# Choosing the experts token tile by token tile, in front of the first tile's last split steps

## The reference, cut to what matters

```python
hf = rmsnorm(x, norm_ffn_g[layer])
logits = (xt @ w_router + b_router).astype(jnp.float32)
top_vals, top_idx = lax.top_k(logits, TOP_K)
gates = jax.nn.softmax(top_vals, axis=-1)
...
gu = xb @ w1[e] + b1[e]
gate = jnp.minimum(gu[:, :F], SWIGLU_LIMIT)
up = jnp.clip(gu[:, F:], -SWIGLU_LIMIT, SWIGLU_LIMIT)
act = (up + 1.0) * gate * jax.nn.sigmoid(SWIGLU_ALPHA * gate)
return act @ w2[e] + b2[e]
```

## Time and profile before

| what | us |
|---|---|
| median of 3 runs | 1243.93 |
| the 3 runs, lowest and highest | 1243.72 and 1245.78 |
| the profiled execution | 1244.29 |
| its span, first to last instruction | 1242.5 |
| PE busy in the span | 1172.0 |
| DVE busy in the span | 373.4 |

### The profile page before, as it was taken

The page is one execution under the profiler, slowest core; times in us unless marked ns, Lnnn a source line. Parts: engine busy times, 40 slices in busy tenths (PEclk is TensorE's granted clock), DMA queues, the critical chain, the costliest instruction groups (busy, mean ns, idle before and its releaser), DMA issues.

```text
span 1242.5 us, 17266 instructions
## 1 busy us (share of the span) xinstructions
PE 1172.0 (94%) x7208; PEld 591.8 (48%) x7208; DVE 373.4 (30%) x677; ACT 228.8 (18%) x342; POOL 58.5 (5%) x39
## 2 busy tenths in 40 slices
PE   9999999999999999999988999999999999989997
PEld 8998888888633333333333333333333333333332
DVE  5655755656522112121111112211112111111112
ACT  5444543544510001000000001000000000000001
POOL 0950000000300000000000000000000000000000
PEclk9999999999999999999999999999999999999999
DMA  9755435947999999999999999999999999999996
GB/s 311 265 203 183 156 136 207 353 152 282 370 422 429 426 429 427 428 428 430 427 428 429 429 428 427 429 430 428 426 430 429 428 428 428 429 430 428 427 426 268
DMA packets 56644, 461.88 MB, mean 372 GB/s; under 512 B 5665, under 2 KB 7394, under 8 KB 31682
## 3 DMA queue, kind: packets, MB, share of 16 engines
q1 hardware_dynamic: 53096, 457.99, 88.8%
q10 hardware_dynamic: 3514, 3.40, 0.9%
HBM read 460.30 MB, written 1.07 MB: 371 GB/s over the span
## 4 chain that ended last, share of the span: by engine, by line
PE 58%; DMA 37%; DVE 1%; SPq 1%; ACT 1%; issue 0%; POOL 0%; DVEq 0%; ACTq 0%
DMA w_ring<-in_w 23%; PE ps L1211 15%; PE ps L1261 11%; DMA behind_xb<-in_w 7%; DMA behind_watt<-in_w 7%; PE ps L1347 3%; PE ps L948 3%; PE ps L946 3%; PE ps L947 3%; PE ps L1189 2%; PE ps L939 2%; PE ps L942 2%; PE ps L941 2%; SPq L553 1%; PE ps L958 1%; PE ps L1084 1%
## 5 line engine op out<-in xcount | busy, mean ns | idle before, releaser
L1211 PE MATMUL ps<-w_ring,A_W 128*64 128x512 f32 x1232 | 278.7, 597 | 32.8 <-DMA w_ring<-in_w 32.5
L1211 PEld LDWEIGHTS ps<-w_ring,A_W 128*64 128x64 f32 x1232 | 84.3, 136 | 204.1 <-issue 141.9
L1757 DVE TENSOR_SCALAR A_W<-ps 128x512 f32<-128x512 f32 x32 | 22.1, 692 | 499.1 <-PE ps L1211 499.1
L1261 PE MATMUL ps<-w_ring,A_W 128*64 128x512 f32 x592 | 134.2, 595 | 0.0
L1424 DVE TENSOR_TENSOR w_parts<-w_ring,w_parts 128x1024 fp32r<-128x1024 f32 x76 | 101.8, 1349 | 86.3 <-ACT w_parts L657 86.0
L853 ACT ACTIVATE A_W<-A_W 128x512 f32<-128x512 f32 x32 | 20.2, 630 | 526.9 <-DVE A_W L1757 526.9
L1211 PE MATMUL ps<-A_QK,A_W 128*64 128x512 f32 x416 | 94.8, 597 | 9.9 <-DMA A_QK<-in_w 9.9
L657 ACT ACTIVATE w_parts<-w_ring 128x1024 fp32r<-128x1024 f32 x76 | 80.1, 1059 | 73.3 <-PE ps L948 37.8
L1261 PEld LDWEIGHTS ps<-w_ring,A_W 128*64 128x64 f32 x592 | 40.3, 136 | 68.6 <-issue 66.9
L857 ACT ACTIVATE A_W<-ps 128x512 f32<-128x512 f32 x31 | 18.5, 597 | 290.8 <-PE ps L1242 290.8
L946 PE MATMUL ps<-w_parts,hT_hi 128*128 128x512 f32 x176 | 69.4, 394 | 0.0
(11 more groups left out here) (255 smaller groups left out, 1263.8 us busy)
## 6 DMA issues: line engine op xcount, KB each, us to landing
w_ring<-in_w SPq DMA_DIRECT2D x113, 2048.0 KB, 43.7
A_QK<-in_w SPq DMA_DIRECT2D x38, 2048.0 KB, 42.8
behind_watt<-in_w SPq DMA_DIRECT2D x19, 2048.0 KB, 43.7
w_ring<-in_w_in SPq DMA_DIRECT2D x36, 1024.0 KB, 7.1
behind_xb<-in_w SPq DMA_DIRECT2D x18, 2048.0 KB, 43.7
w_ring<-in_w_ret_branch SPq DMA_DIRECT2D x2, 2048.0 KB, 12.3
w_ring<-in_w SPq DMA_DIRECT2D x4, 1024.0 KB, 40.1
A_W<-in_w_out SPq DMA_DIRECT2D x1, 2560.0 KB, 14.3
```

What stands on the lines that cost most here:

```text
L1211: mm = pe.matmul(o, XT[:, k, :], tile[:, j, c * HALF:(c + 1) * HALF], start=(k == 0), stop=(k == KC - 1))
L1261: mm = pe.matmul(ps[CAP * c:CAP * c + CAP, 3, :], lhs, w2_tile(flat)[:, q % W2_ROWS, c * HALF:(c + 1) * HALF], start=False, stop=(q == FQ ...
```

## The change

On DVE the choice of experts is made for one tile at a time, and tile 0's choice is put in front of `first_rest(2)` and `first_rest(3)`, which stay in front of tile 1's. The two masks are signalled one by one, and PE's position counts wait for both. The reduction to `mask_f` and the steps behind it stay joint for both tiles. On PE tile 1's logits begin as soon as the first four column blocks are copied, and eight fill matmuls in front of them go. The tile `chosen` moves to words 5888 to 6143 of A_W, away from words 4096 to 4351, which tile 1's transposed columns (xT[1]) still hold at that time.

```diff
-        chosen = A_W[:, 4096:4096 + TT * TOP_K * N_EXP].rearrange("p (t j e) -> p t j e", t=TT, j=TOP_K)
+        chosen = A_W[:, 5888:5888 + TT * TOP_K * N_EXP].rearrange("p (t j e) -> p t j e", t=TT, j=TOP_K)
...
             logits(0, range(4, KC)).then_inc(s_lg, 1)
-            fill(1, 8)
+            pe.wait_ge(s_xte, 3)
+            logits(1, range(4))
             pe.wait_ge(s_xte, 4)
-            logits(1, range(KC)).then_inc(s_lg, 1)
+            logits(1, range(4, KC)).then_inc(s_lg, 1)
             fill(2, 30)
 
-            pe.wait_ge(s_mask, 1)
+            pe.wait_ge(s_mask, TT)
...
             residual_scale(1)
+
+            lg = [top[:, 32 + t * 32:64 + t * 32] for t in range(TT)]
+            best = top[:, 0:16].rearrange("p (t j) -> p t j", t=TT)
+
+            def choose_experts(t):
+                dve.wait_ge(s_lg, t + 1)
+                link(dve.scalar_tensor_tensor(lg[t], ps[:, t, 0:N_EXP], rstd[:, t:t + 1], br_sb[:, :], ALU.mult, ALU.add))
+                link(dve.max(best[:, t, :], lg[t]))
+                link(dve.max_index(ids[:, t, :].bitcast(U32), best[:, t, :], lg[t]))
+                experts = expert_sb[:, :].rearrange("p (a e) -> p a e", a=1).broadcast_to([P, TOP_K, N_EXP])
+                owners = ids[:, t, 0:TOP_K].bitcast(U32).rearrange("p (j a) -> p j a", a=1).broadcast_to([P, TOP_K, N_EXP])
+                link(dve.tensor_tensor(chosen[:, t], experts, owners, ALU.is_equal))
+                dve.tensor_reduce(mask_bf[:, t, :], chosen[:, t].rearrange("p j e -> p e j"), AX.X, ALU.max).then_inc(s_mask, 1)
+
+            choose_experts(0)
             first_rest(2)
             first_rest(3)
-
-            lg = [top[:, 32 + t * 32:64 + t * 32] for t in range(TT)]
-            best = top[:, 0:16].rearrange("p (t j) -> p t j", t=TT)
-            for t in range(TT):
-                dve.wait_ge(s_lg, t + 1)
-                last = dve.scalar_tensor_tensor(lg[t], ps[:, t, 0:N_EXP], rstd[:, t:t + 1],
-                                                br_sb[:, :], ALU.mult, ALU.add)
-            link(last)
-            for t in range(TT):
-                last = dve.max(best[:, t, :], lg[t])
-            link(last)
-            for t in range(TT):
-                last = dve.max_index(ids[:, t, :].bitcast(U32), best[:, t, :], lg[t])
-            link(last)
-            experts = expert_sb[:, :].rearrange("p (a b e) -> p a b e", a=1, b=1).broadcast_to([P, TT, TOP_K, N_EXP])
-            owners = ids[:, :, 0:TOP_K].bitcast(U32).rearrange("p t (j a) -> p t j a", a=1).broadcast_to([P, TT, TOP_K, N_EXP])
-            link(dve.tensor_tensor(chosen, experts, owners, ALU.is_equal))
-            dve.tensor_reduce(mask_bf[:, :, :], chosen.rearrange("p t j e -> p t e j"), AX.X, ALU.max).then_inc(s_mask, 1)
+            choose_experts(1)
             dve.tensor_reduce(mask_f, chosen.rearrange("p t j e -> p t e j"), AX.X, ALU.max).then_inc(s_maskf, 1)
```

## The result

The changed kernel takes 1252.78 us, median of 4 runs (1252.33 to 1252.90), against 1244.14 for the kernel before, median of 4. The medians lie 8.6 us apart, and the measured ratio is 1.0064 with a 95% interval of 1.0052 to 1.0077. The forecast was no change, at 1244.7.

The account below looks back on a forecast made before the run. The full DMA weight stream from unit 10 on was taken as the bound. A store 0.94 us later, less 0.14 filled by the gain's transfer, gave +0.8 us on 1243.93, so 1244.7 us, range 1243.4 to 1245.6.

Parts of the forecast that it names:

- The bound: Weight stream: from unit 10 on only DMA fixes the end; 381.7 MB at 429 GB/s need 889.7 us.
- Nothing else moves.: Outside the routing stage: new place of `chosen` costs no time, SP's queue and the loop stay the same.
- The collisions: Routing stage: DVE's two-input instructions and POOL's exclude each other, store 0.94 us later, 1244.7 us in all; chance 0.50.
- my estimate of 0.28: DVE, routing stage: one tile's comparison over 128 columns takes 0.28 us, upper bound 0.64.
- my 1.54: DVE, routing stage: one tile's choice of experts takes 1.54 us undisturbed, 321.29 to 322.83 for tile 0.
- The clock rival: PE idle 3.3 us before the counts: clock falls, expert 0's first unit takes twice 3.65 us, 1248.4 us; chance 0.04.
- My condition: PE before the counts: clock can fall only after a wait longer than 2.06 us, mask later than 326.2.
- The asymmetry: PE's start of expert 0: earlier gains at most 0.3 us, later costs nearly the full slip.
- The hole: DMA stream before unit 10: gap of some 0.3 us grows by 0.94, less 0.14 filled by the gain's transfer.
- My signs: Profile after: right if the later rate is 427 to 430 GB/s; wrong if granted clock under 1.00 between 327 and 340.
- "Within 0.2%": Whole kernel: time stays within 0.2%, or 2.5 us, of before; chance 0.95, slower 0.04, faster 0.01.
- All rivals: Routing stage: undisturbed 1243.8 us (0.40), fallen PE clock 1248.4 (0.04), whole 0.84 us gained 1243.1 (0.04).

Follow-up runs that it names:

- e5: Kernel before with 24 extra matmuls of 512 columns on ones in each round of PE's expert loop; 1244.29 us, ratio 1.0004.
- e1: Changed kernel with eight more matmuls on ones at the start of PE's program, restoring the loop's old place; 1243.76 us, ratio 1.0001.
- e2: Kernel before with eight fewer matmuls on ones at the start of PE's program, loop at its new place; 1252.55 us, ratio 1.0067.
- e10: Kernel before with 60 memory-to-memory copies of 16 KB, spread over all DMA engines, in ACT's expert loop; 1246.35 us, ratio 1.0019.
- e11: Kernel before with 30 undivided copies of one row of 4099 words in ACT's expert loop; 1259.76 us, ratio 1.0125.
- e4: Changed kernel with the eight fills put back behind tile 1's logits, in PE's idle time; 1243.98 us, ratio 1.0003.
- e3: Changed kernel with only DVE's part kept: PE has its eight fills and tile 1's logits in one piece again; 1244.14 us, ratio 1.0001.
- e6: Kernel before with 48 more matmuls on ones at the start of PE's program; 1244.33 us, ratio 1.0004.
- e8: Kernel before with one matmul on ones fewer at the start of PE's program; 1252.80 us, ratio 1.0071.
- e9: Kernel before with 80 more matmuls on ones at the start of PE's program; 1253.93 us, ratio 1.0074.
- e7: Kernel before with 64 more matmuls on ones at the start of PE's program; 1248.92 us, four runs from 1244.78 to 1251.59.

## Why the prediction was wrong, point by point

**The bound was right.** The DMA stream fixes the end from unit 10 on. e5 confirms it: 15 us more work of PE in 450 us, and no change.

**The step that failed** is the sentence "Nothing else moves. [...] SP's queue and the loop are the same." The loop's code is the same, but its place in PE's program is not. The term was left out altogether: 45 more loads of PE instructions in a stream with no room. e1 and e2 show it from both sides, the loss gone with the place restored, and 8.5 us there with nothing but the place changed. The row on queue 8 stood in the page of before: 26 packets, 0.43 MB, which is PE's built program loaded once although its loop runs six times. I did not ask what keeps a loop of 1670 instructions loaded, nor what would end it.

**The size, worked out.** In the loop the weights fall behind. From 350 to 1200 us the weights' queue and queue 8 moved, in the kernel before and in the changed one:

```profile
q1 hardware_dynamic: 24992, 363.90, 100.6%
q8 instruction: 7, 0.11, 0.1%
```

```profile
q1 hardware_dynamic: 24869, 362.11, 100.2%
q8 instruction: 52, 0.85, 0.4%
```

That is 1.79 MB less of weights for 0.74 MB more of instructions. Over sixteen engines at 429 GB/s 1.79 MB are 4.2 us, which is also what 427 in place of 429 GB/s makes of 381.7 MB (893.9 us against 889.7, both rates rounded). But the end of the stream shows eight engines late and eight in time. Eight engines bring half of 429 GB/s, and at that rate 1.79 MB are 8.3 us, close to the 8.6 measured. That the 45 loads lie on those eight is an inference from the shares of the last windows, since the profile gives a packet no engine. What stays open is why a load displaces 2.4 times its own bytes. In the time of an engine a load costs 8.6 x 8 / 45 = 1.5 us, an undivided copy of the same size 0.52 (15.6 / 30). So its size alone does not explain its price, and e10 and e11 show only that the spread over engines matters (0.04 us a copy, 2.2 / 60, when spread).

**The collisions** were right in kind and three times too large. Timeline of DVE and of POOL in the changed kernel:

```profile
322.53 2.31 DVE L1650 SCALAR_TENSOR_TENSOR A_W<-A_W,small,xs 128x512 f32<-128x512 f32 x2
...
325.56 0.44 DVE L1673 TENSOR_TENSOR A_W<-expert_sb,A_W 128x128 f32<-128x128 f32 x1
```

```profile
322.93 4.09 POOL L614 TENSOR_TENSOR A_W<-A_W,xs 128x512 f32<-128x512 f32 x3 [0.87 <-ACT xs L804]
```

The two first rests took 2.31 us in place of 1.45, 0.86 more, which I read as a wait of one of them for POOL. POOL's three rests took 4.09 in place of 3.77, 0.32 more and not 0.94. I had laid `first_rest(3)` and the comparison end to end with POOL's jobs in full; POOL gave up only 0.32 for both. Tile 1's comparison took 0.44 us beside these rests, over my estimate of 0.28, but far from a wait for a whole job of POOL. Tile 0's choice took 1.69 us (320.93 to 322.62) against my 1.54.

**The clock rival**, at 4 in 100, came true as a mechanism: the mask came after 2.58 us of idle PE and the clock was at its lower level through the gather, 2.74 us in place of 1.57. Its price was wrong. The clock was back when expert 0 began, whose first unit took 3.65 us as before; what it cost was the gather's 1.17 us. Between e1 and e4, where the clock held, no loss can be measured: 1243.76 and 1243.98. My condition, a wait longer than 2.06 us, did not decide either: the clock held after 2.13 (e4) and fell after 2.15 (e3).

**The asymmetry** of the store, hidden if earlier, paid if later, could not be tested finely. The hole that I forecast as 0.8 us is there: from 333 to 338 the changed routing stage brings 300 GB/s (e1) and the old one 372 (e2), a difference of 5 x 72 / 429 = 0.8 us.

```profile
333.00:338.00 5.00, 5.00 (x28) 1.77 (x26) 2.24 (x14) 1.04 (x2) 0.00 (x0) 1.00 0.90 300
```

```profile
333.00:338.00 5.00, 5.00 (x28) 2.07 (x26) 2.08 (x14) 0.55 (x2) 0.00 (x0) 1.00 1.02 372
```

That the size fits is luck: in e1 unit 10 stands 17.56 us behind unit 7's issue against 16.32 before, 1.24 later, and most of it is the clock, since in e4, with the same order and the clock held, it is 0.07 later. Whether the hole reaches the end can't be said: e1 lies within about 0.1% (1.2 us) of the kernel before, on either side.

**My signs.** A clock under 1.00 behind 327, a sign of being wrong outright, came and was not the cause. The rate of 427 GB/s lay in the 427 to 430 that I had given as a sign of being right, with half of the engines falling behind in it.

**"Within 0.2%" at 0.95** was far too sure. All rivals lay in the stage that the change touches; none asked what the removal of instructions does to those that follow.

## What to carry to other kernels

In a program with a large hardware loop, adding or removing instructions anywhere in front of it moves the loop against the blocks in which the program is loaded. Before believing a small difference, compare the packets of the instruction queue in both pages; if they differ, restore the place with padding at the program's start and measure again. And where the DMA stream is the bound, ask over how many engines the small transfers are spread, and not only how many bytes they are; a stream's last microseconds show it.

## What the runs showed of the hardware

- PE's instruction store holds this body of 1670 instructions from round to round when it lies in seven blocks of 256, and loads it anew in every round when it touches an eighth: 26 packets or 71, at 16.4 KB each (before, e6; the changed kernel, e2, e8, e9). With 6 or 7 instructions in the eighth (e7) the runs lay between. The Trainium skill (Runtime: NRT & Kernel Launch, Instruction fetch mechanics) says that PE's instruction memory is 128 KiB, 2048 instructions, filled in blocks of 16 KiB or 256 instructions. Eight blocks with one of them for the block ahead would give the limit seen here; that is argued, not shown. The same section says that only two blocks are kept; in the kernel before a body of seven blocks is run six times with no load between 472 and 1209 us, which speaks against that on PE.
- One matmul fewer in front of the loop cost 0.7% (e8_cut1, 1.0055 to 1.0086).
- With 71 packets the stream ends on eight of the sixteen DMA engines: a share of 0.47 to 0.54 from 1229 to 1237 us (the changed kernel), where the kernel before shows no such step.
- An undivided copy of 16 KB on a single DMA engine cost the full stream 0.52 us, the same bytes spread over all engines 0.04 us (e11, e10).
- The granted clock fell after 2.58 and after 2.15 us of idle PE (e1, e3) and held after 2.13 and 2.06 (e4, e2), so the length of the idle time alone did not decide it here.
